# Where the gather products of a next pair's second row block stand beside the down products

## What is computed

```
h = rms_norm(x)
group = argmax(h @ rg_w + rg_b)             # 4 groups
two experts of the group's 8, weights tw    # 32 experts in all
for each expert e, over its tokens:
    hid = silu(h @ w_gate[e]) * (h @ w_up[e])     # 1024 -> 512
    y   = hid @ w_down[e]                         # 512 -> 1024
    x[token] += tw * y
```

## Time and profile before

| | |
|---|---|
| median of 3 runs | 1393.49 us (1392.65 to 1395.43) |
| span of the profiled execution | 1389.9 us, first to last instruction |
| around the span, against the median | 3.6 us |
| PE busy | 1362.8 us, 98% |
| PE weight loads busy | 807.2 us, 58% |
| DVE busy | 583.7 us, 42% |
| ACT busy | 386.0 us, 28% |
| granted TensorE clock, mean | 0.998 of full speed |
| HBM read | 488 MB, 352 GB/s over the span |

### The profile page before, as it was taken

One profiled execution on the slowest core, in us unless ns is written; L12 is line 12 of the kernel. 1 busy time (PEld: TensorE's weight loads), 2 busy tenths in 40 slices (PEclk: granted clock), 3 DMA queues, 4 the chain that ended last, 5 costly groups with the idle time before them and its releaser, 6 DMA issues. The chain is left out here.

```text
span 1389.9 us, 18890 instructions
## 1 busy us (share of the span) xinstructions
PE 1362.8 (98%) x7854; PEld 807.2 (58%) x7854; DVE 583.7 (42%) x934; ACT 386.0 (28%) x709; POOL 6.3 (0%) x36
## 2 busy tenths in 40 slices
PE   8999999999999999999999999999999999999996
PEld 7899888644444444444488988884444444444432
DVE  7796646642222222212278956467222222222223
ACT  6554444211111111111164553441111111111112
POOL 0000000000000000000000000000000000000000
PEclk9999999999999999999999999999999999999999
DMA  9645758999999999999975557599999999999996
GB/s 310 222 165 186 277 198 317 406 390 428 427 428 429 427 426 428 428 427 420 406 232 187 212 184 270 185 385 386 412 430 427 427 428 428 426 428 426 425 421 250
DMA packets 88524, 490.27 MB, mean 353 GB/s; under 512 B 10558, under 2 KB 13688, under 8 KB 58744
## 3 DMA queue, kind: packets, MB, share of 16 engines
q1 hardware_dynamic: 88336, 489.03, 87.8%
q10 hardware_dynamic: 104, 0.03, 0.0%
HBM read 487.99 MB, written 1.05 MB: 352 GB/s over the span
## 5 line engine op out<-in xcount | busy, mean ns | idle before, releaser
L2083 PE MATMUL psB<-slots,uT 128*64 128x512 f32 x2016 | 456.2, 595 | 4.9 <-DMA slots<-in_expert_w_gate_dram 3.5
L2083 PEld LDWEIGHTS psB<-slots,uT 128*64 128x64 f32 x2016 | 141.6, 137 | 268.1 <-issue 264.6
L2093 PE MATMUL psC<-slots,ybT_plain 128*64 128x512 f32 x1024 | 227.2, 595 | 4.8 <-DMA slots<-in_expert_w_down_dram 4.3
L1196 DVE TENSOR_TENSOR parts<-slots,parts 128x2048 fp32r<-128x2048 f32 (+1 forms) x80 | 177.6, 2249 | 69.9 <-ACT parts L961 69.2
L961 ACT ACTIVATE parts<-slots 128x2048 fp32r<-128x2048 f32 (+1 forms) x80 | 148.3, 1888 | 97.2 <-PE psB L1731 52.7
L1572 DVE TENSOR_TENSOR x<-x,psA 128x1024 f32<-128x1024 f32 x62 | 75.7, 1221 | 216.1 <-PE psA L2133 216.0
L2093 PEld LDWEIGHTS psC<-slots,ybT_plain 128*64 128x64 f32 x1024 | 71.7, 137 | 134.8 <-issue 129.0
L1068 ACT ACTIVATE rel_parts<-psC 128x512 fp32r<-128x512 f32 x62 | 37.0, 597 | 384.6 <-PE psC L2093 205.5
L1731 PE MATMUL psB<-parts,hT_parts 128*128 128x512 f32 x448 | 139.1, 392 | 1.5 <-DVE parts L1196 1.0
L1566 DVE TENSOR_TENSOR rel_parts<-psC,rel_parts 128x512 fp32r<-128x512 f32 x62 | 42.6, 688 | 166.0 <-ACT rel_parts L1068 165.9
L1731 PE MATMUL psA<-parts,hT_parts 128*128 128x512 f32 x320 | 99.3, 392 | 0.0
(11 more groups left out here) (357 smaller groups left out, 1372.8 us busy)
## 6 DMA issues: line engine op xcount, KB each, us to landing
slots<-in_expert_w_gate_dram SPq DMA_DIRECT2D x44, 2048.0 KB, 24.2
slots<-in_expert_w_up_dram SPq DMA_DIRECT2D x44, 2048.0 KB, 23.3
slots<-in_expert_w_down_dram SPq DMA_DIRECT2D x44, 2048.0 KB, 25.1
slots<-in_w_in_dram SPq DMA_DIRECT2D x56, 1024.0 KB, 5.2
slots<-in_expert_w_gate_dram SPq DMA_DIRECT2D x36, 1024.0 KB, 10.4
slots<-in_expert_w_up_dram SPq DMA_DIRECT2D x34, 1024.0 KB, 10.3
slots<-in_expert_w_down_dram SPq DMA_DIRECT2D x28, 1024.0 KB, 11.7
slots<-in_expert_w_down_dram SPq DMA_DIRECT2D x24, 512.0 KB, 9.4
```

The source lines that it names most:

```text
L1196: v.tensor_tensor(low_part, mix_slot(i), high_part, ALU.subtract).then_inc(low_dve, 1)
L2083: ins = te.matmul(psB[j * BLK:(j + 1) * BLK, o, :], xT[:, 4 * half + c, j * BLK:(j + 1) * BLK], w, start=half == 0 and c == order[0], stop ...
L2093: ins = te.matmul(psC[j * BLK:(j + 1) * BLK, n, :], hidT[:, 2 * k + c, j * BLK:(j + 1) * BLK], w[:, c, n * 512:(n + 1) * 512], start=k == ...
```

## The change

`gather` gets an argument that says which of the six terms it runs, and counts up `gather_ps` only when it has run the last one. In `pair`, the second row block's gather is split: terms 0 and 1 (8 products) stay in front of the first down half, and terms 2 to 5 (16 products) stand between the two down halves. All else, the waits too, is as it was.

```diff
-                def gather(b, first=False):
-
-                    for n, (part, t) in enumerate(GATHER_TERMS):
+                def gather(b, first=False, terms=range(len(GATHER_TERMS))):
+
+                    for n in terms:
+                        part, t = GATHER_TERMS[n]
...
-                    ins.then_inc(gather_ps, 1)
+                    if n == len(GATHER_TERMS) - 1:
+                        ins.then_inc(gather_ps, 1)
...
                     if gather_next:
-                        gather(1)
-                    for k in range(2):
-                        pe.wait_ge(hidT_act, g * 2 + k + 1)
-                        down(i, k, tail)
+                        gather(1, terms=range(0, 2))
+                    pe.wait_ge(hidT_act, g * 2 + 1)
+                    down(i, 0, tail)
+                    if gather_next:
+                        gather(1, terms=range(2, len(GATHER_TERMS)))
+                    pe.wait_ge(hidT_act, g * 2 + 2)
+                    down(i, 1, tail)
```

## The result

| | before | after |
|---|---|---|
| median of the runs | 1392.98 us | 1398.84 us |
| span of the profiled execution | 1389.9 us | 1397.1 us |
| PE busy | 1362.8 us | 1372.4 us |
| DVE busy | 583.7 us | 583.4 us |
| first gather to last down products, layer 0 | 254.24 to 684.20: 429.96 us | 255.56 to 688.61: 433.05 us |

The changed kernel is slower: ratio 1.0039, 95% interval 1.0028 to 1.0049, 5.9 us by the medians. The prediction was 1393.6 us, no change. The spans differ by more, 7.2 us, because this execution's layer 0 reached its expert part 1.3 us later, before anything that was changed.

A forecast was written before the change was run, and what follows sets the result against it. The weight stream was taken to bound each layer's end, hiding TensorE's 4.2 us a layer; early and late releases nearly cancelled, +0.1 us for both layers, added to the median: 1393.6 us, range 1391.3 to 1397.0.

The forecast's parts named there:

- What bounds the kernel: End of each layer: set by the stream of weights; TensorE delays inside pairs cost nothing up to about 4.4 us a layer.
- The price of a change of kind: TensorE between the down halves: two more changes of kind cost 0.30 us a pair, 4.2 us a layer.
- The rule cited from the Trainium skill: TensorE pulls weight loads ahead of running matmuls; as a rival, changes of kind are free: 1391.8 us, chance 0.06.
- The cover of the hidden activation's copy: Before the first down half: 8 products instead of 24 still cover ScalarE's copy, no wait, 0.18 us to spare.
- rival A: At the first down half: copy cover too thin, higher price per pair; 0.45 us or more gives 1398.4 us, chance 0.10.
- the second row block's completion: On VectorE's wait: completion comes some 4 us later, the scaled block is needed over 7 us on; cost nothing.
- The size of the gain at pair 0 and of what follows: Stream at pair 0: runs 0.99 us ahead; later releases come 0.30 and 0.60 us late, less the backlogs.
- My estimate of a 2 MB load into an empty queue: Weight stream: a 2 MB load that finds an empty queue lands after about 7.45 us.
- The backlog of 0.75 or 1.15 us: Stream behind pair 0: landing times less 7.45 us leave 0.75 us in layer 0, 1.15 in layer 1, against late releases.
- Idle engines: Weight stream, 997 to 998 us: the dip to 262 GB/s means some of the 16 engines were already empty.
- The other bound: High end: if the dips mean a release already binds, the gain is lost and each layer's stream ends 0.60 us late.
- The sum: Both layers together: the terms' middles, +0.2 and +0.05 us, taken as +0.1 us on the median.

The follow-up runs named there:

- e2_pair0_whole: Changed kernel, but in pair 0 of each layer the second row block's gather stands whole before the down halves again; ratio to the kernel before 1.0007.
- e6_more_price: e1_tables_first plus three more products, whose result nothing reads, between the down halves of pairs 2 to 13; ratio to the kernel before 1.0109.
- e5_pair0_split_tables_first: Kernel before with the gather split in pair 0 of each layer alone, VectorE's overflow tables moved between the two scalings there; ratio to before 1.0011.
- e1_tables_first: Changed kernel, with VectorE computing the overflow tables between the two scalings of gathered rows in pair 0 of each layer; ratio to the kernel before 1.0018.
- e7_singles_longer: Kernel before, with one more pair's worth of slots (12) loaded by single 1 MB loads at a layer's start; ratio to before 0.9992.
- e4_before_dve_held: Kernel before, with VectorE in pair 0 also waiting for the first down half's end before scaling the second row block; ratio to before 1.0034.
- e3_pair0_split_only: Kernel before, with the gather split in pair 0 of each layer alone; ratio to before 1.0032.
- e10_after_singles: Changed kernel with the longer single loads at a layer's start and nothing else; ratio to the kernel before 1.0009.

## Why the prediction was wrong, point by point

- **What bounds the kernel** held. The end of each layer is set by the stream, the waits for weights are the credit, and a delay of TensorE inside it is hidden. e2_pair0_whole shows it for 26 splits, e6_more_price from the other side.
- **The price of a change of kind** held: 0.30 us forecast, 27.38 us a pair measured. The rule cited from the Trainium skill (TensorE: Matmul & The Clock Gate, Part 2), by which the weight load would have hidden it, isn't enough for these two changes of kind: 0.30 us a pair stayed visible.
- **The cover of the hidden activation's copy** held: no idle time in front of the first down half. So rival A, whose 1398.4 us is close to the time measured, is not what happened. The number would have been right for the wrong reason.
- **The step that failed** is the one on VectorE: "the second row block's completion moves behind the first down half ... Free." I read what is queued behind that wait in a steady pair, where it is one rounding with 5 us of idle time ahead of it (the row at 1075.49 us, above). The change also touches pair 0, and there the queue is the tables, four additions and both scatter operands, some 13 us with no idle time noted in it (275.93 to 288.97 us before). The row of VectorE's timeline at 275.93 us was there to be read before. The wait that the change lengthened was priced by the pair that repeats 13 times, not by the one that differs. I put it at nothing; it cost 2.1 us of TensorE in each layer, in the one stretch in which a late release isn't forgiven.
- **The size of the gain at pair 0 and of what follows** was off. I bounded the stream's shift at -0.85 to +0.60 us a layer. The gain at pair 0 is real: the first issue comes 0.98 us sooner, and in e5_pair0_split_tables_first the stream is 1.1 us ahead 30 us into layer 0. But it was lost and more. The layers of that kernel ran 2.4 and 2.9 us longer than before in its trace, part of which is chance (below): its ratio is worth 0.8 us a layer. The term that was mis-sized is what it costs to start again from empty. I took the end of a dry stretch to be the release plus a fixed time, so that being emptier before it could cost no more than the gain. The windows show 35 and 15 GB/s less over 20 us, 1.6 and 0.7 us, for a release only 0.30 us later. My estimate of a 2 MB load into an empty queue, 7.45 us, was close (7.7 us measured). The backlog of 0.75 or 1.15 us, though, was no margin to be spent: with less of it the rate fell.
- **Idle engines** are only a part of that fall. In the changed kernel the DMA share falls with the rate (0.91 and 0.86), but in e1_tables_first and e5_pair0_split_tables_first it stays at 0.98 and 0.99 while the rate is 376 to 394 GB/s. There the 16 engines were at a packet nearly all of the time and carried less with it. Nor did the first two doubled loads land sooner, as they should have from a shorter queue: after 9.3 and 9.1 us in layer 0 of e5_pair0_split_tables_first, 9.1 and 8.2 us before. Why the rate fell there, no run here shows.
- **The other bound**, that the dips to 262 GB/s meant a release was already binding, was the better reading, and e7_singles_longer supports it: with half of each release sooner, the dip is gone and the kernel before is 0.08% faster, at the edge of its interval.
- **The sum** had 0.1 us where 5.9 was right. Of the 0.39%, the tables' place makes 0.21% (1.0039 to 1.0018), and 0.18% is left. The long single loads take that away and 0.14% more (1.0018 to 0.9986); 0.08% of this they give the kernel before too. The wait costs about the same with them, 0.23%, as without them, 0.21%, so no run shows that it costs more where the stream is thin. The split with neither fault costs nothing that can be measured.

What stays open: in single traces, some layers lose 1.2 to 2 us more of the stream than others in their first 25 us, in kernels that do the same there (369 GB/s in layer 1 of e1_tables_first, 398 in its layer 0). Layer 0 of the changed kernel is such a layer, with 380 GB/s where its layer 1 has 403 and both layers before have 396. No run here says what decides it. So the length of a single layer is good to 1 or 2 us at best, and the verdicts above go by the ratios. A trace is also of one execution: that of e5_pair0_split_tables_first took 1399.66 us, where the median of its runs is 1395.42. And why the engines carry less when little is queued stays open, as said above.

## What to carry to other kernels

When a step is moved that another engine waits for, read what is queued behind that wait in every iteration that differs, the first and the last ones above all, and not in the steady one. And where a stream of transfers bounds a stage, look for the few microseconds in which it runs thin. Here a delay elsewhere cost next to nothing as long as the last waits for weights covered it (e2_pair0_whole); in the thin stretch 2.3 us of waits cost 2.4 us a layer (e4_before_dve_held), and a gain ahead of it wasn't kept. That a short delay there costs more than its own length is seen in one trace, not in the times. What helped was to issue smaller transfers as soon as each part of the space was free until the backlog had grown, and to merge them only then.

## What the runs showed of the hardware

The same wait of 1.9 us on TensorE, in the same place, left the granted clock alone in the changed kernel (1.00 in 290 to 300 us), in e3_pair0_split_only and in e4_before_dve_held, but not in e10_after_singles, where it fell in both layers. There the mean over 290 to 295 us was 0.83, so the clock stood at the lower of its two levels, 1.2 GHz, for a part of it, and the next 32 products took 8.02 us where they take 7.09. Timeline of TensorE, and the window:

```profile
292.88 0.47 PE L2134 MATMUL psA<-rel_parts,selT 128*128 128x512 f32 x1 [1.88 <-DVE rel_parts L1566]
...
294.77 8.02 PE L2085 MATMUL psB<-slots,uT 128*64 128x512 f32 x32
```
```profile
290.00:295.00 5.00, 3.12 (x14) 1.37 (x12) 3.09 (x4) 0.12 (x2) 0.00 (x0) 0.83 1.01 428
```

From the end of the wait to the next gather product it took 9.85 us (292.88 to 302.73), where the changed kernel took 8.27 us (294.18 to 302.45). So the same wait of just under 2 us may or may not cost another 1.6 us of slow clock; what decides it no run shows. Part of what e10_after_singles lost in its profiled execution is that.
